# Decoder step with mixture of experts on one core: split first pieces, biases permuted by a transfer, router in four column groups, reordered routing

## What is computed

```python
def layer(x, conv_prev, mk, mv, ...):
    x = x + mixer(rmsnorm(x, g_mix), conv_prev, w_in, ...)        # projections, spatial gate, short conv, w_out
    x = x + cross_attn(rmsnorm(x, g_xattn), mk, mv, w_q, w_xo)    # keys and values of 256 memory tokens
    return x + moe(rmsnorm(x, g_moe), w_router, b_router, w1, b1, w2, b2)

def moe(h, ...):                                  # 32 experts, 4 per token
    logits = h @ w_router + b_router
    top_logit, top_e = lax.top_k(logits, 4)
    gates = softmax(top_logit)
    # per expert e, for its tokens:
    gate, up = split(xb @ w1[e] + b1[e])
    glu = min(gate, 7) * sigmoid(1.702 * gate)
    out += gate_of_token * (((clip(up, -7, 7) + 1) * glu) @ w2[e] + b2[e])
```

## Time and profile before

| | |
|---|---|
| median of 3 runs | 1241.31 us (1238.46 to 1241.55) |
| profiled execution, its own time | 1241.03 us |
| its span, first to last instruction | 1239.2 us |
| TensorE matmuls busy | 1167.4 us (94%) |
| VectorE, ScalarE, GpSimd busy | 282.8, 166.1, 31.9 us |
| mean granted TensorE clock | 0.992 |
| DMA over the span | 458.60 MB, mean 370 GB/s |

### The profile page before, as it was taken

How to read it: one execution, slowest core, us unless ns; L and a number is a source line. 1 busy time by engine, 2 the same in 40 slices (tenths; PEclk the granted TensorE clock), 3 DMA queues, 4 the chain that set the end, 5 groups by cost and what they waited for, 6 DMA issues and landing times.

```text
span 1239.2 us, 15028 instructions
## 1 busy us (share of the span) xinstructions
PE 1167.4 (94%) x6004; PEld 630.5 (51%) x6004; DVE 282.8 (23%) x609; ACT 166.1 (13%) x267; POOL 31.9 (3%) x69
## 2 busy tenths in 40 slices
PE   8999999999999999899999999989999899999995
PEld 7888887774444444344444434433444343334443
DVE  5114532342111111112211111111111111111115
ACT  2011011021111111111111112111111111111112
POOL 1000000010000000000000000000000000000000
PEclk9999999999999999999999999999999999999998
DMA  9953334946999999999999999999999999999991
GB/s 374 406 177 136 128 146 167 427 191 245 415 427 428 426 428 428 426 426 430 426 428 427 426 430 425 427 428 427 427 429 428 425 429 427 428 427 427 428 394 55
DMA packets 37837, 458.60 MB, mean 370 GB/s; under 512 B 5744, under 2 KB 5744, under 8 KB 7056
## 3 DMA queue, kind: packets, MB, share of 16 engines
q1 hardware_dynamic: 35424, 454.11, 87.4%
q10 hardware_dynamic: 2352, 3.54, 0.8%
HBM read 454.41 MB, written 3.23 MB: 369 GB/s over the span
## 4 chain that ended last, share of the span: by engine, by line
DMA 50%; PE 45%; DVE 3%; issue 1%; SPq 0%; ACT 0%; DVEq 0%; ACTq 0%
DMA ring<-in_w_gu 50%; PE ps L1149 16%; PE ps L925 15%; PE ps L1196 5%; PE ps L943 2%; PE ps L1104 1%; PE ps L1124 1%; PE ps L1179 1%; DVE arena L851 1%; DMA ring<-in_w_k 1%; PE ps L1011 1%; PE ps L1042 1%; PE ps L1051 1%; PE ps L1021 1%; DVE arena L863 0%
## 5 line engine op out<-in xcount | busy, mean ns | idle before, releaser
L1149 PE MATMUL ps<-ring,arena 128*64 128x512 f32 x2048 | 457.3, 598 | 41.5 <-DMA ring<-in_w_gu 32.6
L1149 PEld LDWEIGHTS ps<-ring,arena 128*64 128x64 f32 x2048 | 144.3, 138 | 349.0 <-issue 278.6
L1196 PE MATMUL ps<-ring,arena 128*64 128x512 f32 x1024 | 226.8, 595 | 6.2 <-DVE arena L863 6.2
L830 DVE TENSOR_TENSOR resid<-resid,ps 128x264 f32<-128x264 f32 x128 | 51.3, 427 | 726.4 <-PE ps L1124 726.4
L925 PE MATMUL ps<-arena,ring 128*128 128x264 f32 (+1 forms) x832 | 186.6, 386 | 3.1 <-DMA ring<-in_w_k 1.7
L925 PEld LDWEIGHTS ps<-arena,ring 128*128 128x128 f32 x832 | 157.4, 190 | 30.6 <-DMA ring<-in_w_k 2.3
L1196 PEld LDWEIGHTS ps<-ring,arena 128*64 128x64 f32 x1024 | 70.7, 137 | 146.9 <-issue 130.7
L1104 PE MATMUL ps<-arena 128*128 128x128 f32 x816 | 102.6, 283 | 0.2 <-DVE arena L612 0.2
L1104 PEld LDWEIGHTS ps<-arena 128*128 128x128 f32 x816 | 100.0, 198 | 0.7 <-DVE arena L612 0.7
L545 ACT ACTIVATE arena<-ps 128x1024 f32<-128x1024 f32 x32 | 32.8, 1024 | 450.8 <-PE ps L1149 450.8
L1124 PE MATMUL ps<-arena 128*128 128x264 f32 x256 | 72.6, 396 | 0.0
(11 more groups left out here) (190 smaller groups left out, 423.2 us busy)
## 6 DMA issues: line engine op xcount, KB each, us to landing
ring<-in_w_gu SPq DMA_DIRECT2D x128, 2048.0 KB, 24.3
ring<-in_w_dn SPq DMA_DIRECT2D x64, 2048.0 KB, 20.3
ring<-in_w_in SPq DMA_DIRECT2D x10, 1024.0 KB, 27.6
ring<-in_kc SPq DMA_DIRECT2D x8, 1024.0 KB, 4.8
ring<-in_vc SPq DMA_DIRECT2D x8, 1024.0 KB, 4.8
ring<-in_w_v SPq DMA_DIRECT2D x4, 1024.0 KB, 24.0
ring<-in_w_out SPq DMA_DIRECT2D x4, 1024.0 KB, 5.8
ring<-in_w_q SPq DMA_DIRECT2D x4, 1024.0 KB, 4.7
```

The lines of the kernel that those rows point to most:

```text
L830: TTN(resid[:, m, :], resid[:, m, :], ps[:, 6 + m % 2, 0:T], ALU.add).then_inc(c_added, 1)
L1149: last = mm(ps[64 * h:64 * h + 64, n, :], xg[:, cur, k, SLOTS * (j % 2):SLOTS * (j % 2) + SLOTS], w[:, at:at + 512], start=(k == 0), stop= ...
L1196: last = mm(ps[64 * h:64 * h + 64, 4, :], hid[:, k, :], w[:, at:at + 512], start=(k == 0), stop=(k == KT - 1))
```

## The change

Five things change. **First pieces:** `mem` and the first `w_k` chunk come in three pairs of pieces (k tiles 0 to 1, 2 to 3, 4 to 7), alternating on SyncE's queue; TensorE runs both first key groups piece by piece, has 9 warm-up matmuls, and the memory's sum of squares moves behind the third key group. **Biases:** the group `bias` is gone; VectorE splits `b_gu` into a scratch area, and four transfers on ACT's queue, ahead of the two stores of keys and values there, write it back permuted; VectorE waits for them late in the mixer, and the bias add in the loop reads another layout. **Logits:** the eight router matmuls write four column groups, two each; the copy of 128 partitions is turned and summed by three matmuls with a matrix `fold`, which VectorE makes in the attention stage. **Top-k:** the chain up to the selection is shorter, `rank` counts from 1. **Gates:** differences, Exp and gates come after the slot matrix; the first gather comes before the gates' transpose, and the register load of `iters` between them; the second gather's copy is waited for inside the loop.

```diff
+FIRST_PARTS = [(0, 2), (2, 4), (4, 8)]
-            for half in range(2):
-                sp.dma_start(mem_raw[:, 4 * half:4 * half + 4, :], mem_t[:, 4 * half:4 * half + 4, :]).then_inc(mem_in[half], 16)
-                sp.dma_start(ring[:, 0, 1024 * half:1024 * half + 1024],
-                             w_k[0, :, 1024 * half:1024 * half + 1024]).then_inc(landed[0] if half else half_landed, 16)
+            for part, (k, k_end) in enumerate(FIRST_PARTS):
+                sp.dma_start(mem_raw[:, k:k_end, :], mem_t[:, k:k_end, :]).then_inc(mem_in[part], 16)
+                sp.dma_start(ring[:, 0, 256 * k:256 * k_end], w_k[0, :, 256 * k:256 * k_end]).then_inc(
+                    landed[0] if part == 2 else part_landed[part], 16)
...
+            act.wait_ge(bias_split, 1)
+            width = P // ROWS_DN
+            for q in range(ROWS_DN):
+                rows = par_of("b_gu")[width * q:width * q + width, :].rearrange("p (j n) -> p j n", j=ROWS_DN)
+                act.dma_start(rows, b_split[:, q].rearrange("p e b -> p (e b)")).then_inc(bias_in, 16)
...
-                if n == 3:
-                    act.wait_ge(ex_in, 1)
-                    nc.scalar.activation(ex[:], ex[:], ACT.Exp).then_inc(ex_out, 1)
...
+            act.wait_ge(ex_in, 1)
+            nc.scalar.activation(ex[:], ex[:], ACT.Exp).then_inc(ex_out, 1)
...
-            copy(b_gu.rearrange("p e h (b j) -> p j e h b", j=ROWS_DN),
-                 filled("bias").rearrange("p (j e h b) -> p j e h b", j=ROWS_DN, e=NE, h=2)).then_inc(emptied, 1)
+            copy(b_split[:], b_gu.rearrange("p e h (b q) -> p q (e h) b", q=ROWS_DN)).then_inc(bias_split, 1)
...
+            dve.wait_ge(bias_in, 16 * ROWS_DN)
             for m in range(4):
                 projected(12 + m)
...
-                        bias = b_gu[:, bass.ds(expert0 + j, 1), h, :].rearrange("p a m -> p (a m)")
-                        TTN(both[:, :, h, :], turned[:, :, h, :], bc(bias, 2, [P, KT, SLOTS]),
-                            ALU.add).then_inc(t_read, 1)
+                        bias = b_tiles[:, :, bass.ds(expert0 + j, 1), h, :].rearrange("p m a b -> p (a b) m")
+                        TTN(both[:, :, h, :].rearrange("p (b m) s -> p b m s", b=2),
+                            turned[:, :, h, :].rearrange("p (b m) s -> p b m s", b=2),
+                            bc(bias, 3, [P, 2, ROWS_DN, SLOTS]), ALU.add).then_inc(t_read, 1)
...
+            keep_busy(ps[:, 7, :], 9)
+            first_keys = ring[:, 0, :].rearrange("p (k n) -> p k n", k=KT)
+            for part, (k_first, k_end) in enumerate(FIRST_PARTS):
+                pe.wait_ge(landed[0] if part == 2 else part_landed[part], 16)
+                for m in range(2):
+                    for k in range(k_first, k_end):
+                        pe.wait_ge(mem_ready, k + 1)
+                        last = mm(bank(("k", m))[:, 0:NMEM], first_keys[:, k, P * m:P * m + P], mem[:, k, :],
+                                  start=(k == 0), stop=(k == KT - 1))
...
-                last = mm(b[0:NE, 0:T], router[:, k, :], h_fm[:, k, :], start=(k == 0), stop=(k == KT - 1))
+                part = NE * (k % 4)
+                last = mm(b[part:part + NE, 0:T], router[:, k, :], h_fm[:, k, :], start=(k < 4), stop=(k >= 4),
+                          tile_position=(0, part))
...
-                last = turn(b[:, NE * t:NE * t + NE], lT[:, P * t:P * t + P], ident[0:NE, 0:NE])
+                last = mm(b[:, NE * t:NE * t + NE], lT[:, P * t:P * t + P], fold[:], start=True, stop=True)
...
             b = begin("rank")
+            keep_busy(b, 2)
             pe.wait_ge(sel_ready, 1)
...
+            pe.wait_ge(late_zero, 5)
+            pe.wait_ge(tok_copied, 6)
+            b = begin(("ga", 0))
+            keep_busy(b, 2)
+            gather(b, 0, begun=True).then_inc(grp, 1)
+            pe.wait_ge(iters_ready, 1)
+            end = pe.value_load(iters[0:1, 0:1], min_val=4, max_val=20)
             b = begin("gT")
             pe.wait_ge(gate_ready, 1)
...
-            pe.wait_ge(emptied, NG)
+            pe.wait_ge(emptied, NG - 1)
...
+                        if j == 0 and u == 2:
+                            pe.wait_ge(emptied, NG)
```

More of the change, by code:

```diff
@@ L261, in build @@
         late_zero = sem("late_zero")
+        first_p = sem("first_p")
+        top_filled = sem("top_filled")
         p_built = sem("p_built")
@@ L886, in _, with keep_busy @@
             mm, turn = nc.tensor.matmul, nc.tensor.transpose
+            def keep_busy(b, n):
+                for _ in range(n):
+                    mm(b[:, 0:P], ones[:], ones[:], start=True, stop=True)
             def begin(name):
@@ L930, in _ @@
             pe.wait_ge(const_ready, 3)
-            for _ in range(12):
-                mm(ps[:, 7, 0:P], ones[:], ones[:], start=True, stop=True)
-            for m in range(KT):
-                project("w_k", m, lambda k: mem[:, k, :], "k", (mem_ready, 0) if m == 0 else None)
-                if m == 1:
+            keep_busy(ps[:, 7, :], 9)
[7 more added lines that the diff above has]
+                                  start=(k == 0), stop=(k == KT - 1))
+                    if part == 2:
+                        last.then_inc(grp, 1)
+            for m in range(2, KT):
+                project("w_k", m, lambda k: mem[:, k, :], "k")
+                if m == 2:
                     pe.wait_ge(const_ready, CONSTS)
@@ L1092, in _, with gather @@
             last.then_inc(grp, 1)
+            def gather(b, n, begun=False):
+                for part in range(4):
+                    first = 512 * n + 256 * (part // ROWS_GU) + part % ROWS_GU
+                    for t in range(TT):
+                        if begun:
+                            pe.wait_ge(p_built if t == 2 else first_p, 1 if t == 2 else t + 1)
+                        last = mm(b[:, P * part:P * part + P], h_tok[:, t, first:first + ROWS_GU * (P - 1) + 1:ROWS_GU], p_hot[:, t, :],
+                                  start=(t == 0), stop=(t == TT - 1))
+                return last
+            pe.wait_ge(late_zero, 5)
[5 more added lines that the diff above has]
+            end = pe.value_load(iters[0:1, 0:1], min_val=4, max_val=20)
             b = begin("gT")
```

120 lines of the change are left out of this document (50 added, 70 removed).

## The result

The changed kernel takes 1229.4 us (median of 4 runs, 1228.44 to 1230.66) where the kernel before takes 1240.78 us beside it (4 runs, 1238.46 to 1241.55): ratio 0.9908, 95% interval 0.9894 to 0.9923. It is faster by more than the 0.3% that a measurement here can tell. The prediction was 1231.9 us with a range of 1229 to 1237. The profiled execution took 1230.66 us, its span is 1228.9 us, and the mean granted clock is 0.991.

A forecast was written before the change was run, and what follows sets the result against it. The expert stage was taken as bound by weight transfers, its start hanging on TensorE; terms -1.8 - 2.0 - 2.4 - 0.9 - 0.4 - 1.9 = -9.4 from 1241.03 give 1231.6, plus 0.3 for the median: 1231.9 us, range 1229 to 1237.

The forecast's parts named there:

- First pieces, −1.8: Kernel start: 16 instead of 24 matmuls behind the last first-weight piece, saving 1.8 us; far end 0.8 us of delay.
- rival (b): First transfers: the pieces cost what they bring, so the 1.8 us gain shrinks to nothing; 1233.7 us, chance 0.10.
- Biases, −2.0: Between values and input projection: the bias piece leaves TensorE, saving 2.0 us; its replacement costs zero.
- Up to the first gather, −2.4: Router to first gather: shorter logits, selection chain and copies start the gather 2.4 us earlier; ends -1.8 and -3.2.
- Gathers at full clock, −0.9: The two gathers: no TensorE pause ahead, so full instead of half clock, saving 0.9 us; ends 0 and -1.2.
- clock at the first expert, −1.9: First expert's 64 instructions: shorter pauses keep the clock full, 13.76 instead of 15.64 us; ends 0 and -1.9.
- Rival (a): Routing and loop entry: the clock still falls, both clock terms go, 1234.7 us; chance 0.25.
- Load, gates, entry, −0.4: Last gather to first expert: load 1.1, transposes 0.35, entry 0.25, 1.7 us for 2.1; ends -1.0 and +0.5.
- In the loop, 0: Expert loop: the bias add reads the same number of elements, so no change in time.
- rival (d): Expert loop: the bias add's new read pattern becomes the bound; at three times its price 1263 us, chance 0.03.
- Rival (c): Front: its 3.8 us are lost to a later wait and the clock falls too; 1238.5 us, no difference, chance 0.07.

The follow-up runs named there:

- before_again: The kernel before the change, unedited, run and profiled a second time: 1240.1 us (10 runs), ratio 0.9996; profiled execution 1238.37 us.
- again: The changed kernel run a second time with nothing edited: 1229.42 us, ratio to the kernel before 0.9908.
- no_fill: The changed kernel without the filling matmuls ahead of the ranks and of the first gather: 1230.81 us, ratio to the kernel before 0.9921.
- bare_long: The changed kernel without filling matmuls and with four chained, unused VectorE operations added ahead of the selection: 1231.73 us, ratio to the kernel before 0.9931.
- wait_all: The changed kernel with the wait for the second gather's copy back ahead of the expert loop, load still between the gathers: 1230.91 us, ratio 0.992.
- load_late: The changed kernel with the register load moved behind the second gather, right ahead of the loop, wait still inside it: 1229.82 us, ratio 0.9912.
- bias_pe: The changed kernel with the biases permuted by TensorE again and the loop's old bias add: 1232.4 us, ratio to the kernel before 0.9932.
- entry_old: The changed kernel with both the second gather's copy wait and the register load right ahead of the loop, as before: 1232.48 us, ratio 0.9936.

## Why the prediction was right, and where its steps were not

The path was right: everything ahead of SyncE's first issue for expert 1 moved the end by as much as it moved that issue. The issue moved by 9.66 us and the span by 10.3. The sum, −9.4, came out at −10.3 in one pair of profiles and −8.3 in the other. The median moved by 11.4 us, to 2.5 below the forecast and 0.4 above the low end of the range. The terms were less good than their sum. Of the marks that it named, the loop's start (276.8 us, 277.3 named) and the issue (280.65, 280.9) came out; the second key group (15.1 us, 13.4 named) and the first gather (270.74, 269.6) did not.

- **First pieces, −1.8.** The step said that two more pieces delay nothing and that the last piece lands as early as the last half did. It failed: TensorE went on at 11.51 and 10.55 us, and after 10 us in all profiles with three pairs, which is the sign that the prediction set for rival (b); the halves let it go on at 9.76 and 9.58. On average the delay is 1.0 us, where the far end of the step was 0.8, and 0.7 us of 1.8 were kept (14.95 to 14.21), between forecast and rival (b). The first profile alone shows rival (b) whole, at 0.0. The step gave the two more issues on SyncE's queue no time; the last one now goes out 0.95 us later (3.15 us, 2.20 before). What gave −1.5 in both of its profiles is TensorE's new order with the two old pairs, which the prediction did not price apart from the number of pieces.
- **Biases, −2.0.** Right in mechanism, 2.2 in size; where the 0.2 beside the piece itself lie was not followed up. The four issues took 2.95 us on ACT's queue and the copy 1.84 us of VectorE, both beside TensorE, as forecast.
- **Up to the first gather, −2.4.** It was −2.9. The column groups gave 1.8, the low end of the step. From the router's start to the end of the selection the working gave 6.4 us (264.33 to 270.7), and 6.59 were measured (262.13 to 268.46 + 0.26). Behind it the working gave 2.7 us and 2.02 were measured. The part that was too careful is TensorE's stretch ahead of the ranks: it was to end 0.6 us behind the selection, but transposes and fillers end at 268.68 us (268.07 + 0.61), and the selection at 268.72, so nothing was lost there.
- **Gathers at full clock, −0.9, and clock at the first expert, −1.9.** In the profile of before the falls cost 0.96 us (6.88 against 5.92 in `before_again`) and 1.7 (15.64 against 13.95), the size of the two terms. The mechanism was read rightly in that profile, but the step from one profile to the kernel failed: `before_again` has no fall, and there both terms are 0. Rival (a), that the clock still falls, was wrong for the changed kernel: 1.00 in all windows from 264 to 285 us, and gathers and first expert of the same length in `again`. The Trainium skill, "TensorE: Matmul & The Clock Gate", part 4 on PE-mode transpose, says that a transpose does not count as busy in the way that a matmul does; by that rule the first gather would be slow after 24 transposes. It was at full clock there in `no_fill` with no fillers, in `before_again` too, and slow in `bare_long`, where a pause of 1.80 us came on top. No run here removes the transposes, so what share they have in the falls is not shown.
- **Load, gates, entry, −0.4.** This is the term that was mis-sized: −1.95, measured between two profiles without a fall, and beyond its far end of −1.0. The step took the old pause of 2.10 us to be copy 0.73, load 1.1 and entry 0.25, and moved the load to a place where it would still cost 1.1. In fact the pause is the wait for the copy with the branch behind it (1.28 us, `wait_all`) and the load between them (0.8). Where TensorE's queue holds matmuls ahead of it, the load takes no time that the trace shows (`load_late`, 0.0), presumably because it is done while they still run. The new pauses of 1.1 and 0.3 us that the prediction expected do not exist.
- **In the loop, 0.** The bias add costs what it did, 688 ns, so rival (d) is out. But the stretch behind the first issue is 0.5 to 0.6 us shorter than before in both pairs. To TensorE's last wait for weights it is 1.0 to 1.1 us shorter, and part of that is given back at the very end (last section). `bias_pe`, with the old layout, has a long stretch too, longer than before's. So some of the gain may come with the new layout, in a place where the prediction put nothing. What links the layout of the biases with a stage bound by transfers is open: from 470 to 1185 us the rate reads 427 GB/s in all of them, and nothing was tried on it.
- **Rival (c)**, that the front's gain is lost to a later wait, is out: from the second key group to the router no stretch got longer.

So the forecast met the time partly by luck, because errors cancelled: first pieces worth 1.1 us less than thought, entry 1.5 us more, and 2.8 us of clock terms that hold for some executions of before and not for others.

The best version by the marks is the changed kernel with two pairs: first issue for expert 1 at 279.02 and 278.97 us, against 280.65 and 279.69. By its times (1228.94 and 1229.05 us) it beats the kernel before by as much as the changed kernel does, and is not told from the latter.

## What to carry to other kernels

Take a wait on work that has just been started, and a register load behind it, away from the head of a loop: let the engine enter with its queue full and wait at the first instruction that needs the result. Here that is worth 2.0 us, and the load by itself nothing. Before splitting a first transfer further, reorder its consumer so that the first part covers the second's landing; more pieces can land later. And profile the unchanged kernel twice before a clock fall in one profile becomes a term of a sum.

## What the runs showed of the hardware that was not expected

**The granted clock differs between executions of one program at the same pause.** At a pause of 2.1 us ahead of the first expert it fell in one profile of before and not in the other, nor in `entry_old`; no fall followed 1.28 us (`wait_all`) and 1.20 us; behind 1.80 us (`bare_long`) it fell, and ahead of the ranks 1.58 us stand in both profiles of before, one with a fall and one without. The final sum of squares, two instructions after a pause of 3.9 us, shows it best, since its instructions are the same in all kernels. From the timelines of `before_again`, `again` and `wait_all`:

```profile
1227.54 0.71 PE L1206 MATMUL ps<-ssum,ones 128*128 128x264 f32 x2 [3.90 <-DVE ssum L598]
```

```profile
1218.66 1.23 PE L1227 MATMUL ps<-ssum,ones 128*128 128x264 f32 x2 [3.91 <-DVE ssum L608]
```

```profile
1221.83 0.71 PE L1225 MATMUL ps<-ssum,ones 128*128 128x264 f32 x2 [3.90 <-DVE ssum L608]
```

The same two instructions take 0.71 us in three of the 14 profiles and 1.23 to 1.25 in nine, with a granted clock of 1.00 in `before_again` and 0.53 in `again` over their length; in the two left, between. This is the half microsecond that `again` gives back at the end against `before_again`.

**The first transfers land with a scatter of over a microsecond.** With three pairs, TensorE's next piece starts between 13.78 and 15.06 us in nine profiles of nearly the same program; with two pairs it hardly moves (13.43, 13.40), because TensorE is then busy until after the landing. In these two profiles the covered wait took the scatter away with it.
